# The key half of a cross attention's projection, computed three stages earlier and parked in DRAM

## The chip, the cores and the metric

The kernel runs on one core of one Trainium2 chip. The metric is device time in microseconds of one launch. Five engines run their own instruction streams in order and meet only through semaphores: TensorE (PE, matmuls), VectorE (DVE), ScalarE (ACT), GpSimd (POOL) and SyncE (SP, which here only issues the weight loads). The DMA engines move data beside them.

## What is computed

Two transformer blocks on 256 tokens of width 2048, all in float32. The parts that matter here, in the order of the kernel's stages:

```python
mix = concatenate([rmsnorm(u, conv_out_norm), rmsnorm(attn, attn_out_norm)]) @ w_out     # stage w_out
x = x + rmsnorm(mix, post_mix_norm)                                                      # the addition after it
hf = rmsnorm(x, pre_ffn_norm)
ff = (silu(hf @ w_gate) * (hf @ w_up)) @ w_down                                          # ffn, down
x = x + rmsnorm(ff, post_ffn_norm)
...                                            # qkv_a, mix2b (delta rule, block attention), w_out_2
q = rmsnorm_2(x, xattn_norm_g) @ w_xq          # stage xq
kv = rmsnorm_2(mem, mem_norm_g) @ w_xkv        # stage xkv: mem is an input, 256 x 2048
k, v = split(kv)                               # 4 heads of 128 each
o = softmax(q k^T * 128**-0.5) v               # cross attention
x = x + o @ w_xo                               # xo, then ffn_2, down_2
```

`mem` is an input, so keys and values of the cross attention depend on nothing that the kernel computes before.

## The kernel before

Every product is a `Gemm` object in the list `GEMMS`. It has groups of weight tiles; one tile is 512 rows by 512 columns of a weight (1 MB), and it is worked off as two units of 256 rows each. A float32 product is made from split operands: `split_act` (L441) writes the rounded high part `w_hi` of a unit on ACT, `split_dve` (L447) writes the rest `w_lo` on DVE, and PE multiplies high by both parts of the activations and low by the high part. The high parts go through a ring of `HIS = 4` units: ACT cannot split unit u before PE has finished unit u-4. The raw tiles go through a ring of `RAW = 4` tiles that SP fills in the order of `GEMMS`.

Activations are split in the same way into `x2` (tile `x` in the trace) by `prep_act` (L923, L925: high parts, "rows" below) and `prep_dve` (L938, L940: low parts), two of the 16 chunks of 128 channels at a time. `square_act` (L969) and `reduce_dve` (L688, L690) gather the sum of squares for a norm, four chunks at a time; PE adds over partitions with a matmul against ones (L1029, L1050, L1060, L1063); `root` (ACT, L1081 to L1084) and `refine` (DVE, L1095 to L1107) make the reciprocal root. The scale of a norm is applied to a product's columns when they leave the accumulator, so a product may start before its norm is known; the addition after w_out may not, since the residual stream must be finished first.

The order on ACT and DVE is written out by hand in their blocks. `ahead` splits units 0 to 2 of the next product, evicts the last group of the one before and splits unit 3; `run`/`turn` split the others, one at a time, and call one step of a `filler` generator after each. Two places matter.

Between w_out and the gate (the first group of ffn), PE's last w_out unit is followed by the sums for the norm "mix". Then `refine` and `add_norm` on DVE scale the product (L2252), add it to `xt` (L2433) and write the low parts of `x2`, while `ready_act` does ACT's share. PE's first gate unit needs the first two chunks of `x2`, each later one two more.

In xkv both halves are multiplied from `xm2` (tile `xm` in the trace), the split `mem`, which is prepared during w_out_2: first the keys, as a wide group of four tiles (L799, L802), then the values in swapped form (L785 to L788). The filler there is `prep_steps_act` and `prep_steps_dve` for "xq": eight steps, each of two chunks of the finished `xt` with its squares, one step after each split from unit 4 on. Nothing of it can start before w_out_2 has ended, since `x2` is in use until then and `xt` is not final. Stage xq follows, and needs those chunks. POOL issues the load of `mem` (L2293), and the small transfers that turn the norm's row into a column for the values (`column_pool`, L1540, L1542).

Of the kernel before, what the change touches and what calls it, by code (L numbers as in the profile page):

```python
# [17 lines left out]
F32 = mybir.dt.float32  # L18
# [6 lines left out]
P = 128  # L25
T = 256
# [118 lines left out]
def build(nc, A, out):  # L145
    with ExitStack() as ctx:
# [68 lines left out]
        wide_tmp = sb("wide_tmp", [P, 8, T], F32, a_gate)  # L215

        XK, XVN, XQ, XO = 0, 8, 12, 16
        XM = 20
# [49 lines left out]
        def x2c(k):  # L268
            return x2[:, k]

        def h2c(k):
# [11 lines left out]
                           for h0, n, off, width, at in ((0, 4, 0, 128, 0), (4, 4, 0, 128, 4), (0, 8, 128, 64, 8))],  # L283
# [3 lines left out]
                            for h0 in (4, 0)],  # L287
# [17 lines left out]
                 x2c, rs_x, form="narrow", column=1),  # L305
            Gemm("w_out_2", 2, [group(w_loop(A["w_out_2"], b * P, 2 * W), 4, out=(xt, 0 + b, 8), kind="add")
                        for b in (0, 4)], x2c),
            Gemm("xkv", 1, [group(w_cols(A["w_xkv_2"], 0, W), 4, out=(ar, XK, 0)),
                           group(w_cols(A["w_xkv_2"], W, W), 4, out=(ar, XVN, XH // 2), kind="v")], lambda k: xm2[:, k], rs_x, column=2),
            Gemm("xq", 1, [group(w_cols(A["w_xq_2"], 0, W), 4, out=(ar, XQ, 0))], x2c, rs_x),  # L310
            Gemm("xo", 1, [group(w_cols(A["w_xo_2"], 512 * n, W), 1, out=(xt, 4 * n, 0), kind="add")
                           for n in range(4)], x2c),
# [12 lines left out]
        for n, g in enumerate(GEMMS):  # L325
            g.before = GEMMS[n - 1] if n else None
            g.u0, g.p0, g.e0, g.g0, g.f0, g.slot0 = tiles, prods, ops, groups, hidden, list(slots)
            at = 0
            g.per_unit = []
            if g.name not in ("latents", "ukv", "down", "down_2"):  # L330

                side = 1 if g.name in ("uq", "qkv_a") else 0
            for k, gr in enumerate(g.groups):
                gr["form"] = "swap" if gr["kind"] == "v" else g.form
                gr["t"], gr["e"], gr["n"] = at, 2 * k, k - (3 if g.name == "w_out" else 0)
                if gr["banks"] is None:
# [24 lines left out]
            hidden += g.turns if g.name.startswith("ffn") else 0  # L361
# [195 lines left out]
        def evict_dve(dve, g, i, gr):  # L557
# [197 lines left out]
        def multiply(pe, g, *stats, between=None, filler=None, at=FIRST + 1):  # L755
# [70 lines left out]
            if between:  # L826
                at, extra = between
                body(0, 0, at)
                extra()
                body(0, at)  # L830
            elif g.name == "w_out":
                at = g.units - 2
                body(0, 0, at)
                pe.wait_ge(geared, 12)
                sum_rows(pe, "mix")
                body(0, at)
                sum_quarter(pe, "mix", STATS["mix"][2] - 1)
            else:
                body(0)
            if g.name in STREAM_STAT and g.turns == 2:  # L840
# [23 lines left out]
        for name, n, first in [("x", 16, 0), ("q", 6, 0), ("kv", 4, 6), ("attn", 8, 8), ("conv", 8, 0),  # L864
                               ("ffn", 16, 0), ("mix2", 16, 0), ("gdn", 8, 0), ("moba", 8, 8), ("mem", 16, 0),
                               ("xq", 16, 0), ("xo", 4, 0), ("ffn2", 16, 0)]:
            PREPS[name] = (sum(c for _, c, _ in PREPS.values()), n, first)
# [23 lines left out]
            return lambda k: (x_lo, off + min(k, total))  # L891

        for name, preps in [("conv_in", ["x"]), ("latents", ["x"]), ("uq", ["q"]), ("ukv", ["kv"]),
                            ("w_out", ["attn", "conv"]), ("ffn", ["ffn"]), ("qkv_a", ["mix2"]), ("mix2b", ["mix2"]),
                            ("w_out_2", ["gdn", "moba"]), ("xkv", ["mem"]), ("xq", ["xq"]),
                            ("xo", ["xo"]), ("ffn_2", ["ffn2"])]:
            G[name].needs = needs_of(*preps)
# [9 lines left out]
            halves += g.turns * g.halves  # L907


        PREP_TO = {"mem": xm2, "q": xq1}  # L910

        def prep_act(act, name, src, gain, ready=None, square=None, after=None, c0=0, count=None):

# [96 lines left out]

        SUM_AT = {"kv": 2, "mean": 2}

        SUM_BANK = {name: 3 if name in ("q", "kv", "mix", "ff", "mix2", "final") else 7 for name in STATS}
        POST_GAIN = {"mix": "post_mix", "ff": "post_ffn"}

        def sum_out(name):
# [1255 lines left out]
        def _(pool):  # L2272
# [53 lines left out]
        def _(act):  # L2326
# [39 lines left out]
            filler = conv_norms_act(act)  # L2366
            next(filler)
            run_("w_out", filler)
            ahead_("ffn")
            root(act, "mix")  # L2370
            ready_act(act, "ffn", gain_of("pre_ffn"), lambda c: (x_added, c + 1), "w_out", G["ffn"])
            run_("ffn", stat=["ffn"], done=DC // 2)
            ahead_("down")
            run_("down")
            ahead_("qkv_a")
# [13 lines left out]
            run_("w_out_2", prep_steps_act(act, "mem", mem_src, gain_of("mem"), lambda c: (mem_in, 16),  # L2389
                                           first=(x_lo, PREPS["moba"][0] + PREPS["moba"][1])))  # L2390
            ahead_("xkv")
            filler = prep_steps_act(act, "xq", xs, gain_of("xattn"), banks_out("w_out_2"), "w_out_2")
# [22 lines left out]
        def _(dve):  # L2415
# [38 lines left out]
                assert apply.n == n0 + ADDS  # L2454


            for u in range(DC // 2):
                split_dve(dve, G["conv_in"], 0, u)
                if u == 0:
# [23 lines left out]
            filler = conv_norms_dve(dve)  # L2483
            next(filler)
            run_("w_out", filler)
            ahead_("ffn")
            add_norm("mix", mix_out, "ffn", "pre_ffn", G["ffn"])
            run_("ffn", stat=["ffn"], done=DC // 2)
            ahead_("down")
            run_("down")  # L2490
            ahead_("qkv_a")
# [39 lines left out]
        def _(pe):  # L2531
# [29 lines left out]
            attention_pe(pe, ATTN["cross"], [lambda e: e.wait_ge(*groups_out("xq")()), lambda e: e.wait_ge(*all_evicted("xkv")())])  # L2561
# [59 lines left out]
```

## Time and profile before

| | us |
|---|---|
| median of three runs | 2622.0 (2620.73 to 2622.4) |
| the profiled execution | 2621.72 |
| its span, first to last instruction | 2619.9 |
| PE busy in the span | 2520.7 (96%) |
| DVE busy | 1658.8 (63%) |
| ACT busy | 1266.8 (48%) |
[...]

The span is cut into 40 slices of 65.5 us in the page's second section; PE stands at 8 or 9 tenths in every one. Times below are us from the span's start. w_out runs from 302 to 407, the gate starts at 417.8, xkv runs from 1736.2 to 1782.5 and xq follows. A number in brackets at the end of a timeline row is the engine's idle time before the row, with the instruction that ended it. Rows of one kind overlap by some 0.1 us in the trace, so the distance between two starts is what an instruction costs in a sequence; it is shorter than the printed duration.

### The profile page before, as it was taken

To read this page: it belongs to the slowest core of one execution; us is meant where nothing else is said; L and a number is where in the kernel's file an instruction comes from. 1 tells how busy PE (TensorE), PEld (TensorE's weight loads), DVE (VectorE), ACT (ScalarE), POOL (GpSimd) and SP (SyncE) were. 2 spreads that over 40 slices of the span, in tenths; PEclk is the share of its full clock that TensorE was granted. 3 is DMA by queue.
4 is the path that set the end of the run, shared out by engine and by line. 5 is a ranking of instruction groups with operands and counts; after the bars stand their busy time and mean duration, and the time that the engine had idled before them with its cause. 6 is when DMAs were issued, how large, how long until landed. Compare 5 with 4: busy or idle time off the path is not lost.

```text
span 2619.9 us, 37766 instructions
## 1 busy us (share of the span) xinstructions
PE 2520.7 (96%) x14866; PEld 2210.0 (84%) x14866; DVE 1658.8 (63%) x2173; ACT 1266.8 (48%) x1627; POOL 62.7 (2%) x57
## 2 busy tenths in 40 slices
PE   8999898999999999989999999998999999999997
PEld 7877697888888888878889989886888888888886
DVE  6898756666656554547776436765767676665454
ACT  5455555444444443445453345654644545444342
POOL 0000000000000000000003210000000000000000
PEclk9999899999999999999999999999999999999999
DMA  6553144655565555544542235453455555565553
GB/s 240 176 145 113 49 158 132 193 183 186 191 191 185 185 192 176 193 161 154 183 164 97 97 121 177 161 181 125 153 186 191 192 184 186 190 192 187 183 184 122
DMA packets 236033, 436.26 MB, mean 167 GB/s; under 512 B 14408, under 2 KB 32856, under 8 KB 235792
## 3 DMA queue, kind: packets, MB, share of 16 engines
q1 hardware_dynamic: 232384, 423.66, 49.9%
q0 software_dynamic: 2240, 6.80, 0.8%
q10 hardware_dynamic: 1296, 4.19, 0.4%
q8 instruction: 82, 1.34, 0.2%
q14 instruction: 31, 0.25, 0.0%
HBM read 432.51 MB, written 3.69 MB: 166 GB/s over the span
## 4 chain that ended last, share of the span: by engine, by line
PE 88%; DVE 7%; ACT 3%; issue 1%; DMA 1%; SPq 0%; DVEq 0%; ACTq 0%
PE ps L799 46%; PE ps L802 23%; PE ps L808 3%; PE ps L810 3%; PE ps L811 3%; DVE w_lo L447 2%; DVE ar L1219 1%; PE ps L1479 1%; PE ps L785 1%; ACT w_hi L441 1%; PE ps L788 1%; PE ps L787 1%; PE ps L1252 1%; PE ps L2086 1%; PE ps L2092 1%
## 5 line engine op out<-in xcount | busy, mean ns | idle before, releaser
L447 DVE TENSOR_TENSOR w_lo<-w_raw,w_hi 128x1024 fp32r<-128x1024 f32 (+3 forms) x820 | 994.3, 1217 | 774.4 <-ACT w_hi L441 772.3
L799 PE MATMUL ps<-x,w_hi 128*128 128x512 f32 x4064 | 1289.4, 399 | 44.5 <-issue 19.4
L441 ACT ACTIVATE w_hi<-w_raw 128x1024 fp32r<-128x1024 f32 (+3 forms) x820 | 853.4, 1045 | 921.8 <-PE ps L802 801.9
L802 PEld LDWEIGHTS ps<-x,w_lo 128*128 128x128 f32 x4064 | 769.9, 189 | 182.9
L802 PE MATMUL ps<-x,w_lo 128*128 128x256 f32 x4064 | 803.3, 279 | 0.0
L799 PEld LDWEIGHTS ps<-x,w_hi 128*128 128x128 f32 x4064 | 625.1, 190 | 48.3 <-issue 36.7
L799 PE MATMUL ps<-h,w_hi 128*128 128x512 f32 x1408 | 444.2, 397 | 4.3 <-DVE w_lo L447 4.3
L802 PEld LDWEIGHTS ps<-h,w_lo 128*128 128x128 f32 x1408 | 265.4, 188 | 62.9
L802 PE MATMUL ps<-h,w_lo 128*128 128x256 f32 x1408 | 277.3, 278 | 0.0
L799 PEld LDWEIGHTS ps<-h,w_hi 128*128 128x128 f32 x1408 | 215.0, 189 | 5.1 <-DVE w_lo L447 4.9
L808 PE MATMUL ps<-x,w_hi 128*128 128x256 f32 x640 | 188.5, 294 | 8.1 <-issue 6.3
L810 PE MATMUL ps<-x,w_hi 128*128 128x256 f32 x640 | 182.8, 286 | 0.0
L811 PE MATMUL ps<-x,w_lo 128*128 128x256 f32 x640 | 182.7, 286 | 0.0
L487 ACT ACTIVATE half<-ps 128x512 f32<-128x512 f32 (+1 forms) x162 | 94.4, 592 | 91.6 <-PE ps L802 91.6
L808 PEld LDWEIGHTS ps<-x,w_hi 128*128 128x128 f32 x640 | 124.7, 195 | 13.6 <-issue 10.3
L810 PEld LDWEIGHTS ps<-x,w_hi 128*128 128x128 f32 x640 | 124.7, 195 | 0.3
L811 PEld LDWEIGHTS ps<-x,w_lo 128*128 128x128 f32 x640 | 124.5, 195 | 0.0
L1219 DVE SCALAR_TENSOR_TENSOR ar<-ar,cols 128x255 f32<-128x255 f32 (+29 forms) x180 | 73.7, 467 | 0.6
L925 ACT ACTIVATE x<-xt,cols 128x256 fp32r<-128x256 f32 x80 | 35.5, 496 | 26.4 <-DVE xt L2433 26.4
L940 DVE SCALAR_TENSOR_TENSOR x<-xt,cols,x 128x256 fp32r<-128x256 f32 x80 | 34.8, 480 | 3.8 <-ACT x L925 3.8
L620 DVE TENSOR_TENSOR up<-half,ps 128x512 f32<-128x512 f32 x44 | 30.1, 684 | 10.9 <-ACT half L487 10.9
L620 DVE TENSOR_TENSOR gate<-half,ps 128x512 f32<-128x512 f32 x44 | 30.0, 684 | 10.5 <-ACT half L487 10.5
(307 smaller groups left out, 1710.5 us busy)
## 6 DMA issues: line engine op xcount, KB each, us to landing
w_raw<-in_w_gate SPq DMA_DIRECT2D x88, 1024.0 KB, 5.1
w_raw<-in_w_up SPq DMA_DIRECT2D x88, 1024.0 KB, 5.2
w_raw<-in_w_down SPq DMA_DIRECT2D x88, 1024.0 KB, 5.1
w_raw<-in_w_in SPq DMA_DIRECT2D x79, 1024.0 KB, 5.1
w_raw<-in_w_out SPq DMA_DIRECT2D x32, 1024.0 KB, 5.1
w_raw<-in_w_xkv SPq DMA_DIRECT2D x8, 1024.0 KB, 5.0
w_raw<-in_w_uq SPq DMA_DIRECT2D x18, 256.0 KB, 3.7
w_raw<-in_w_ukv SPq DMA_DIRECT2D x16, 256.0 KB, 3.9
```

The lines of the kernel that those rows point to most:

```text
L441: nc.scalar.activation(w_hi[:, u % HIS, 0:ks.stop - ks.start, cs], w_raw[:, slot(g, j), ks, cs], ACT.Copy)\
L447: nc.vector.tensor_tensor(w_lo[:, slot(g, j), ks, cs], w_raw[:, slot(g, j), ks, cs], w_hi[:, u % HIS, 0:ks.stop - ks.start, cs].bitcast(F3 ...
L487: nc.scalar.activation(half[:, c:c + n, h], banks[:, :, h], ACT.Copy).then_inc(half_out, 1)
L620: nc.vector.tensor_tensor(dst(c, n)[:, :, h], half[:, c:c + n, h], banks[:, :, T + h.start:T + h.stop], ALU.add)\
L799: nc.tensor.matmul(bank, w_h(k, cs), x(k).rearrange("p a n -> p (a n)"), start=(n == 0 and k == 0), stop=False)
L802: ins = nc.tensor.matmul(bank[:, T:2 * T], w_l(k, cs), x(k)[:, 0, :], start=False, stop=(final and k == ks.stop - 1))
L808: nc.tensor.matmul(out_m, w_h(k, cs), x(k)[:, 0, :], start=(first and k == 0 and m % 2 == 0), stop=False)
L810: nc.tensor.matmul(out_m, w_h(k, cs), x(k)[:, 1, :], start=False, stop=False)
L811: ins = nc.tensor.matmul(out_m, w_l(k, cs), x(k)[:, 0, :], start=False, stop=(final and k == ks.stop - 1 and last_m))
L925: ins = nc.scalar.activation(x2[:, first + c, 0, :], src(c), ACT.Copy, scale=gain(c))
L940: ins = nc.vector.scalar_tensor_tensor(x2[:, first + c, 1, :], src(c), gain(c), hi, ALU.mult, ALU.subtract)
L1219: nc.vector.scalar_tensor_tensor(y[:, s:T], u[:, 0:T - s], w, y[:, s:T], ALU.mult, ALU.add).then_inc(tap1, 1)
```

## The change

The keys' product becomes a stage of its own, `xk`, between w_out and ffn. For it `mem` is loaded once more, earlier (a POOL DMA of 2 MB after the first attention), and split into `xm2` by eight filler steps at the end of w_out. The product is evicted without a scale (kind "raw") to `ar`, written by POOL to a DRAM tensor `xk_d` (512 KB), and read back during w_out_2. After the xq steps DVE multiplies it by `rs_x`, the reciprocal root of mem's norm, which is only computed in xkv. `mem` is loaded and split a second time for the values. Stage xkv keeps four tiles. ACT and DVE wait for the end of the write to DRAM (`xk_out`) before gate unit 5, because ffn's hidden activations overwrite the place. The addition after w_out, `add_norm("mix", ...)`, is replaced by `add_mix`, with the splits of xk's units 4 to 7 and the gate's units 0 to 4 between its parts. The sums of "mix" follow xk's unit 0 on PE. Bank assignments of some products and sums swap sides.

```diff
+            Gemm("xk", 1, [group(w_cols(A["w_xkv_2"], 0, W), 4, out=(ar, XS, 0), kind="raw")], lambda k: xm2[:, k]),
...
-            Gemm("xkv", 1, [group(w_cols(A["w_xkv_2"], 0, W), 4, out=(ar, XK, 0)),
-                           group(w_cols(A["w_xkv_2"], W, W), 4, out=(ar, XVN, XH // 2), kind="v")], lambda k: xm2[:, k], rs_x, column=2),
+            Gemm("xkv", 1, [group(w_cols(A["w_xkv_2"], W, W), 4, out=(ar, XVN, XH // 2), kind="v")], lambda k: xm2[:, k], rs_x, column=2),
...
-                side = 1 if g.name in ("uq", "qkv_a") else 0
+                side = 1 if g.name in ("uq", "ffn", "qkv_a", "xq") else 0
...
+        def w_out_act(act):
+
+            yield from conv_norms_act(act)
+            for c in range(0, DC, 2):
+                prep_act(act, "memk", mem_src, gain_of("mem"), lambda c: (mem_in, 16), None, None, c, 2)
+                yield
...
+            pool.wait_ge(conv_pe, 2)
+            pool.wait_ge(x_lo, PREPS["attn"][0] + PREPS["attn"][1])
+            pool.dma_start(ar[:, MEM:MEM + DC, :], A["mem"]).then_inc(mem_in, 16)
+            pool.wait_ge(evicted, G["xk"].e0 + 2)
+            pool.dma_start(xk_d, ar[:, XS:XS + XH, :]).then_inc(xk_out, 16)
...
+            pool.wait_ge(applied, gated_done)
+            pool.wait_ge(xk_out, 16)
+            pool.dma_start(ar[:, XK:XK + XH, :], xk_d).then_inc(xk_back, 16)
             column_pool(pool, 2, rs_x, "mem")
...
+            g, nxt = G["xk"], G["ffn"]
+            split_act(act, g, 0, 4)
             root(act, "mix")
...
+            rows(0, 2, "w_out")
+            for u in range(5, 8):
+                split_act(act, g, 0, u)
+                rows(2 * u - 8, 2)
+            square_act(act, "ffn", 0, xs, 4)
+            for u in range(4):
+                if u == FIRST:
+                    finish(evict_act(act, g, 0, g.groups[-1]))
+                split_act(act, nxt, 0, u)
+                rows(8 + 2 * u, 2)
+                if u % 2:
+                    square_act(act, "ffn", 1 + u // 2, xs, 4)
+            split_act(act, nxt, 0, 4)
+            square_act(act, "ffn", 3, xs, 4)
+            act.wait_ge(xk_out, 16)
+            run_("ffn", stat=["ffn"], done=5)
...
+                split_dve(dve, g, 0, 4)
+                refine(dve, "mix")
+                add(0, 2)
+                low(0, 2)
+                split_dve(dve, g, 0, 5)
+                add(2, 2)
+                low(2, 2)
+                split_dve(dve, g, 0, 6)
+                add(4, 4)
+                low(4, 2)
+                split_dve(dve, g, 0, 7)
+                low(6, 2)
+                split_dve(dve, nxt, 0, 0)
+                add(8, 4)
+                low(8, 2)
+                reduce_dve(dve, "ffn", 0, 4)
+                split_dve(dve, nxt, 0, 1)
+                low(10, 2)
+                split_dve(dve, nxt, 0, 2)
+                add(12, 2)
+                low(12, 2)
+                finish(evict_dve(dve, g, 0, g.groups[-1]))
+                reduce_dve(dve, "ffn", 1, 4)
+                split_dve(dve, nxt, 0, FIRST)
+                add(14, 2)
+                low(14, 2)
+                reduce_dve(dve, "ffn", 2, 4)
+                split_dve(dve, nxt, 0, 4)
...
             run_("xkv", filler, stat=["mem"])
             finish(filler)
+            dve.wait_ge(xk_back, 16)
+            k = ar[:, XK:XK + XH, :]
+            nc.vector.tensor_tensor(k, k, bc(rs_x, XH), ALU.mult).then_inc(xk_scaled, 1)
             ahead_("xq")
...
+            multiply(pe, G["xk"], between=(1, lambda: sum_quarter(pe, "mix", STATS["mix"][2] - 1)))
             multiply(pe, G["ffn"], "ffn", at=DC // 2)
```

DVE's program in stage xkv before, from the reciprocal root of mem's norm on (`x_50` is `x2`, two chunks a step; `gate` and `up` hold squares; L620 and L631 evict and scale the keys):

```order
L1107 SCALAR_TENSOR_TENSOR rs_x<-st_v,st_y 128x256
L447 TENSOR_TENSOR w_lo<-w_raw,w_hi 128x1024
L940 SCALAR_TENSOR_TENSOR x_50<-xt,cols,x_50 128x256 x2
L447 TENSOR_TENSOR w_lo<-w_raw,w_hi 128x1024
L940 SCALAR_TENSOR_TENSOR x_50<-xt,cols,x_50 128x256 x2
L688 TENSOR_TENSOR up<-up 128x512
L690 TENSOR_TENSOR ssq<-up 128x256
L447 TENSOR_TENSOR w_lo<-w_raw,w_hi 128x1024
L940 SCALAR_TENSOR_TENSOR x_50<-xt,cols,x_50 128x256 x2
L447 TENSOR_TENSOR w_lo<-w_raw,w_hi 128x1024
L940 SCALAR_TENSOR_TENSOR x_50<-xt,cols,x_50 128x256 x2
```

And the same place after the change, from the second pair of chunks behind the root on:

```order
L941 SCALAR_TENSOR_TENSOR x_50<-xt,cols,x_50 128x256 x2
L690 TENSOR_TENSOR up<-up 128x512
L692 TENSOR_TENSOR ssq<-up 128x256
L941 SCALAR_TENSOR_TENSOR x_50<-xt,cols,x_50 128x256 x4
L690 TENSOR_TENSOR gate<-gate 128x512
L692 TENSOR_TENSOR ssq<-gate 128x256
L941 SCALAR_TENSOR_TENSOR x_50<-xt,cols,x_50 128x256 x4
L690 TENSOR_TENSOR up<-up 128x512
L692 TENSOR_TENSOR ssq<-up 128x256
L2603 TENSOR_TENSOR ar<-ar,rs_x 128x1024
L447 TENSOR_TENSOR w_lo<-w_raw,w_hi 128x1024 x3
```

The last eight chunks, their reduces and the keys' scale now stand in one piece after xkv's last split and ahead of xq's first.

DVE's program between w_out and the gate before, from the first addition of four chunks on:

```order
L2252 TENSOR_TENSOR ar<-ar,st_y 128x1024
L2433 TENSOR_TENSOR xt<-xt,ar 128x1024
L940 SCALAR_TENSOR_TENSOR x_50<-xt,cols,x_50 128x256 x4
L2252 TENSOR_TENSOR ar<-ar,st_y 128x1024
L2433 TENSOR_TENSOR xt<-xt,ar 128x1024
L940 SCALAR_TENSOR_TENSOR x_50<-xt,cols,x_50 128x256 x2
L447 TENSOR_TENSOR w_lo<-w_raw,w_hi 128x1024
L940 SCALAR_TENSOR_TENSOR x_50<-xt,cols,x_50 128x256 x2
L447 TENSOR_TENSOR w_lo<-w_raw,w_hi 128x1024
```

And after the change, from the same addition on:

```order
L2269 TENSOR_TENSOR ar<-ar,st_y 128x1024
L2511 TENSOR_TENSOR xt<-xt,ar 128x1024
L941 SCALAR_TENSOR_TENSOR x_50<-xt,cols,x_50 128x256 x2
L447 TENSOR_TENSOR w_lo<-w_raw,w_hi 128x1024
L941 SCALAR_TENSOR_TENSOR x_50<-xt,cols,x_50 128x256 x2
L447 TENSOR_TENSOR w_lo<-w_raw,w_hi 128x1024
L2269 TENSOR_TENSOR ar<-ar,st_y 128x1024
L2511 TENSOR_TENSOR xt<-xt,ar 128x1024
L941 SCALAR_TENSOR_TENSOR x_50<-xt,cols,x_50 128x256 x2
L690 TENSOR_TENSOR gate<-gate 128x512
L692 TENSOR_TENSOR ssq<-gate 128x256
L447 TENSOR_TENSOR w_lo<-w_raw,w_hi 128x1024
```

Of the splits there, the first is xk's unit 7, the second the gate's unit 0 and the third the gate's unit 1; before, the two splits are the gate's units 4 and 5, since units 0 to 3 were split ahead of the addition.

## Rows read from the trace of the kernel before

**Rows 1.** PE's timeline at the gate: start, us, instruction, idle before.

```profile
407.47 1.98 PE L1050 MATMUL ps<-up,ones 128*128 128x256 f32 x8
417.81 1.19 PE L799 MATMUL ps<-x,w_hi 128*128 128x512 f32 x2 [8.36 <-issue]
...
422.96 0.62 PE L799 MATMUL ps<-x,w_hi 128*128 128x512 f32 x2
...
443.82 1.89 PE L1060 MATMUL ps<-up,ones 128*128 128x256 f32 x8
```

**Rows 2.** DVE's timeline from the end of w_out to the gate's unit 5.

```profile
411.12 0.42 DVE L1095 TENSOR_SCALAR st_v<-ps 128x256 f32<-128x256 f32 x1
...
413.84 0.42 DVE L2252 TENSOR_TENSOR ar<-ar,st_y 128x256 f32<-128x256 f32 x1
...
415.84 0.68 DVE L2252 TENSOR_TENSOR ar<-ar,st_y 128x512 f32<-128x512 f32 x1
...
423.77 1.22 DVE L2252 TENSOR_TENSOR ar<-ar,st_y 128x1024 f32<-128x1024 f32 x1
425.10 1.23 DVE L2433 TENSOR_TENSOR xt<-xt,ar 128x1024 f32<-128x1024 f32 x1
426.90 0.88 DVE L940 SCALAR_TENSOR_TENSOR x<-xt,cols,x 128x256 fp32r<-128x256 f32 x2 [0.58 <-ACT x L925]
428.25 1.23 DVE L447 TENSOR_TENSOR w_lo<-w_raw,w_hi 128x1024 fp32r<-128x1024 f32 x1 [0.47 <-ACT w_hi L441]
429.39 0.87 DVE L940 SCALAR_TENSOR_TENSOR x<-xt,cols,x 128x256 fp32r<-128x256 f32 x2
...
431.32 0.69 DVE L688 TENSOR_TENSOR gate<-gate 128x512 f32<-128x512 f32 x1
...
432.38 1.22 DVE L2252 TENSOR_TENSOR ar<-ar,st_y 128x1024 f32<-128x1024 f32 x1
```

**Rows 3.** ACT's timeline beside it.

```profile
426.36 0.91 ACT L925 ACTIVATE x<-xt,cols 128x256 fp32r<-128x256 f32 x2 [2.07 <-DVE xt L2433]
```

**Rows 4.** PE's timeline in w_out, at a short wait.

```profile
347.01 0.39 PE L808 MATMUL ps<-x,w_hi 128*128 128x256 f32 x1 [1.79 <-DVE w_lo L447]
```

**Rows 5.** Stretches: us; busy PE, PEld, DVE, ACT, POOL; PEclk; DMA share; GB/s.

```profile
350.00:351.00 1.00, 1.00 (x7) 1.00 (x6) 0.36 (x1) 0.00 (x0) 0.00 (x0) 0.50 0.00 0
350.00:390.00 40.00, 40.00 (x332) 40.00 (x331) 19.21 (x20) 22.31 (x32) 0.00 (x0) 0.99 0.48 159
```

**Rows 6.** PE's timeline in xkv.

```profile
1736.20 0.63 PE L799 MATMUL ps<-xm,w_hi 128*128 128x512 f32 x2
...
1747.34 1.89 PE L1029 MATMUL ps<-ssq,ones 128*128 128x256 f32 x8
1748.89 0.81 PE L799 MATMUL ps<-xm,w_hi 128*128 128x512 f32 x2
...
1760.22 0.40 PE L785 MATMUL ps<-w_hi,xm 128*128 128x512 f32 x1
...
1782.53 0.62 PE L799 MATMUL ps<-x,w_hi 128*128 128x512 f32 x2
```

**Rows 7.** DVE's timeline in xkv.

```profile
1758.08 1.22 DVE L447 TENSOR_TENSOR w_lo<-w_raw,w_hi 128x1024 fp32r<-128x1024 f32 x1
...
1764.13 1.28 DVE L620 TENSOR_TENSOR ar<-half,ps 128x512 f32<-128x512 f32 x2
```

**Rows 8.** ACT's timeline in xkv.

```profile
1755.14 1.04 ACT L969 ACTIVATE up<-xt 128x1024 f32<-128x1024 f32 x1
```

**Rows 9.** PE's timeline at w_out's start.

```profile
302.44 0.55 PE L808 MATMUL ps<-x,w_hi 128*128 128x256 f32 x1 [6.27 <-issue]
...
306.82 0.28 PE L811 MATMUL ps<-x,w_lo 128*128 128x256 f32 x1
```

**Rows 10.** The page's sixth section, DMA issues: KB each, us to landing.

```profile
out_t<-tx ACTq DMA_DIRECT2D x4, 512.0 KB, 2.6
masks_s<-in_masks POOLq DMA_DIRECT2D x1, 512.0 KB, 4.5
```

More of the change, by code:

```diff
@@ L217, in build @@
         XK, XVN, XQ, XO = 0, 8, 12, 16
-        XM = 20
+        XS = 16
         rel_hot = sb("rel_hot", [BUCKETS, 384], F32, a_gate)
@@ L621, in evict_dve @@
                     .then_inc(evicted, 1)
+            if kind == "raw":
+                return
             if kind == "sum":
@@ L836, in multiply @@
                 body(0, at)
-                sum_quarter(pe, "mix", STATS["mix"][2] - 1)
             else:
@@ L863, in build @@
         PREPS = {}
-        for name, n, first in [("x", 16, 0), ("q", 6, 0), ("kv", 4, 6), ("attn", 8, 8), ("conv", 8, 0),
+        for name, n, first in [("x", 16, 0), ("q", 6, 0), ("kv", 4, 6), ("attn", 8, 8), ("conv", 8, 0), ("memk", 16, 0),
                                ("ffn", 16, 0), ("mix2", 16, 0), ("gdn", 8, 0), ("moba", 8, 8), ("mem", 16, 0),
@@ L893, in build @@
         for name, preps in [("conv_in", ["x"]), ("latents", ["x"]), ("uq", ["q"]), ("ukv", ["kv"]),
-                            ("w_out", ["attn", "conv"]), ("ffn", ["ffn"]), ("qkv_a", ["mix2"]), ("mix2b", ["mix2"]),
+                            ("w_out", ["attn", "conv"]), ("xk", ["memk"]), ("ffn", ["ffn"]), ("qkv_a", ["mix2"]), ("mix2b", ["mix2"]),
                             ("w_out_2", ["gdn", "moba"]), ("xkv", ["mem"]), ("xq", ["xq"]),
@@ L907, in build @@
             halves += g.turns * g.halves
-        PREP_TO = {"mem": xm2, "q": xq1}
+        PREP_TO = {"mem": xm2, "memk": xm2, "q": xq1}
         def prep_act(act, name, src, gain, ready=None, square=None, after=None, c0=0, count=None):
@@ L1011, in build @@
         SUM_AT = {"kv": 2, "mean": 2}
-        SUM_BANK = {name: 3 if name in ("q", "kv", "mix", "ff", "mix2", "final") else 7 for name in STATS}
+        SUM_BANK = {name: 4 if name == "mix" else 3 if name in ("q", "kv", "ffn", "mix2", "xq", "final") else 7 for name in STATS}
         POST_GAIN = {"mix": "post_mix", "ff": "post_ffn"}
@@ L1533, in build @@
         mask_in = sem("mask_in")
+        xk_d = nc.dram_tensor("xk_d", [P, XH, T], F32, kind="Internal").ap()
+        xk_out, xk_back, xk_scaled = sem("xk_out"), sem("xk_back"), sem("xk_scaled")
         rs_d = nc.dram_tensor("rs_d", [3, T], F32, kind="Internal").ap()
@@ L2247, in attention_rest_dve, with w_out_dve @@
                 yield
+        def w_out_act(act):
[3 more added lines that the diff above has]
+                yield
+        def w_out_dve(dve):
+            yield from conv_norms_dve(dve)
+            for c in range(0, DC, 2):
+                prep_dve(dve, "memk", mem_src, gain_of("mem"), None, c, 2)
+                yield
         def apply(dve, src, n, first=0):
@@ L2293, in _ @@
             pool.dma_start(ar[:, MEM:MEM + DC, :], A["mem"]).then_inc(mem_in, 16)
+            gated_done = 6 + 2 * ADDS + 2
+            pool.wait_ge(applied, gated_done)
+            pool.wait_ge(xk_out, 16)
+            pool.dma_start(ar[:, XK:XK + XH, :], xk_d).then_inc(xk_back, 16)
             column_pool(pool, 2, rs_x, "mem")
@@ L2365, in _ @@
             prep_act(act, "attn", attn_src, gain_of("attn_out"), lambda c: (applied, 1 if c < 2 else 2), None, "ukv")
-            filler = conv_norms_act(act)
+            filler = w_out_act(act)
             next(filler)
             run_("w_out", filler)
-            ahead_("ffn")
+            finish(filler)
+            ahead_("xk")
+            g, nxt = G["xk"], G["ffn"]
+            split_act(act, g, 0, 4)
             root(act, "mix")
-            ready_act(act, "ffn", gain_of("pre_ffn"), lambda c: (x_added, c + 1), "w_out", G["ffn"])
-            run_("ffn", stat=["ffn"], done=DC // 2)
+            rows = lambda c, n, after=None: prep_act(act, "ffn", xs, gain_of("pre_ffn"), lambda c: (x_added, c + 1), None, after, c, n)
+            rows(0, 2, "w_out")
[14 more added lines that the diff above has]
+            run_("ffn", stat=["ffn"], done=5)
             ahead_("down")
@@ L2388, in _ @@
             prep_act(act, "moba", moba_src, lambda c: col("moba_norm"), lambda c: (hn_used, 16))
-            run_("w_out_2", prep_steps_act(act, "mem", mem_src, gain_of("mem"), lambda c: (mem_in, 16),
+            run_("w_out_2", prep_steps_act(act, "mem", mem_src, gain_of("mem"), lambda c: (mem_in, 32),
                                            first=(x_lo, PREPS["moba"][0] + PREPS["moba"][1])))
@@ L2454, in add_norm, with add_mix, add @@
                 assert apply.n == n0 + ADDS
+            def add_mix():
+                g, nxt = G["xk"], G["ffn"]
+                low = lambda c, n: prep_dve(dve, "ffn", xs, gain_of("pre_ffn"), None, c, n)
+                def add(c0, n):
+                    dve.wait_ge(geared, c0 + n)
+                    apply(dve, mix_out, n, c0)
+                    x = xt[:, c0:c0 + n, :]
+                    nc.vector.tensor_tensor(x, x, span(mix_out, c0, n), ALU.add).then_inc(x_added, n)
+                n0 = apply.n
+                split_dve(dve, g, 0, 4)
[26 more added lines that the diff above has]
+                split_dve(dve, nxt, 0, 4)
+                assert apply.n == n0 + ADDS
             for u in range(DC // 2):
@@ L2482, in _ @@
             prep_dve(dve, "attn", attn_src, gain_of("attn_out"))
-            filler = conv_norms_dve(dve)
+            filler = w_out_dve(dve)
             next(filler)
             run_("w_out", filler)
-            ahead_("ffn")
-            add_norm("mix", mix_out, "ffn", "pre_ffn", G["ffn"])
-            run_("ffn", stat=["ffn"], done=DC // 2)
+            finish(filler)
+            ahead_("xk")
+            add_mix()
+            dve.wait_ge(xk_out, 16)
+            run_("ffn", stat=["ffn"], done=5)
             ahead_("down")
@@ L2560, in _ @@
             pe.wait_ge(st_done, STATS["xq"][0] + 1)
-            attention_pe(pe, ATTN["cross"], [lambda e: e.wait_ge(*groups_out("xq")()), lambda e: e.wait_ge(*all_evicted("xkv")())])
+            attention_pe(pe, ATTN["cross"], [lambda e: e.wait_ge(*groups_out("xq")()), lambda e: e.wait_ge(*all_evicted("xkv")()),
+                                             lambda e: e.wait_ge(xk_scaled, 1)])
             multiply(pe, G["xo"])
```

## The prediction, written before the changed kernel ran

> **What bounds the kernel now.** The table of the page first: PE is busy for 96% of the span, so the time is PE's work plus PE's gaps, and a change that leaves PE's work alone can only win or lose gaps. So the second view is PE's timeline at the two places where the keys' product leaves and arrives. Between w_out and the gate the sums for the norm run from 407.47, and the first gate matmul starts at 417.81 after 8.36 us of idleness [rows 1]. Around it there is more. The clock is low when PE returns: the first 5.15 us (417.81 to 422.96) carry four groups of matmuls that at full clock take an eighth of 22.3 us, 2.8 us, so 2.4 us are lost. A unit costs 2.79 us ((1747.34 - 1736.20)/4, [rows 6]); eight take 22.3, but the gate's eight last 26.0 (417.81 to 443.82), so 1.3 us more go into a later wait. The whole stretch from 407.47 to 443.82 is 36.35 us, with 22.3 of work in it [rows 1]. At the other place there is no gap: the keys run from 1736.20 and, after the sums (1.55 us), to 1760.22, the values to 1782.53, and xq follows at once [rows 6].
>
> **What moves on PE.** The keys' 22.3 us leave xkv and come in behind w_out. Nothing is added to PE's work. Two questions remain: how much of the gap they fill, and whether xkv's other half still covers what the keys covered there.
>
> **Place one, the gate.** DVE has a serial chain here, and the change puts more into it than it takes out of PE's way. Prices in a sequence, by starts: reciprocal root 2.72 (411.12 to 413.84); an addition of four chunks 2.56 (423.77 to 425.10 + 1.23), of two 1.47 (two instructions of the length of the one at 415.84, with their link); after an addition ends, the low parts of two chunks and one split take 3.06 (426.33 to 429.39), since both wait for ACT in turn; a split alone 1.14; two low parts alone 0.8; a reduce 1.06 (431.32 to 432.38) [rows 2]. On ACT two high parts take 0.8 in a sequence, and a square or split 0.95 [rows 3, 8]. The eviction of the keys takes 1.2 [rows 7].
>
> The chain starts later than before. xk's unit 4 can be split only when PE has finished unit 0, at 407.47 + 2.79 = 410.3; ACT and then DVE split it, and DVE reads the sum at 412.75 instead of 411.12. First addition at 415.5. From there, in the written order: add 2, low and split (xk 5) to 420.0; the same (xk 6) to 424.5; add 4, low and split (xk 7) to 430.15; low; the gate's unit 0 is split by 432.85, after ACT's square. Then add 4, low, reduce, split of gate unit 1: 439.0. Low and the split of unit 2, again behind an ACT square: 441.15. Add 2, low, eviction, reduce, split of unit 3: 447.4. Add 2, low, reduce behind the third square, split of unit 4: 452.95.
>
> PE beside it: xk 0 to 410.3, sums to 411.8, xk 1 to 6 without a stop to 428.6, 1.5 us of waiting for xk 7, done at 432.95, gate 0 to 435.75; then 3.2 us, 2.85 us and 2.75 us of waiting before gate units 1, 3 and 4. From unit 4 on the splits come every 1.14 us, faster than PE's 2.79, so gate unit 8's place is reached at 452.95 + 4 x 2.79 = 464.1. With 22.3 us more work, break-even would be 443.82 + 22.3 = 466.1. So the gap of 8.4 us is filled, but it comes back in four pieces, and the gain is 2.0 us at full clock.
>
> Do the pieces cost the clock too? [...] The price lies between 0 and the 2.4 us of the gap before; I take 1.0. [...] Gain at place one: 1.0, with -3 to +5 as its bounds (other rounding of ACT's and DVE's hand-overs, some 0.3 us at each of ten).
>
> Other parts at this place. The eight added steps of `mem` at the end of w_out cost DVE and ACT some 7 us each, where both are busy only 19 and 22 of 40 us and PE waits for neither [rows 5]: nothing; without that cover it would be 7. The load of 2 MB runs beside weight loads at a DMA share of 0.48 over that stretch: nothing, at most 2 us if a tile came late. The write of 512 KB starts after the eviction at 445.2. Its price isn't in the trace; 512 KB landed in 2.6 us from ACT's queue and 4.5 from POOL's [rows 10]. So it ends at about 450, before ACT and DVE reach the wait at 452.7 and 453. Behind the wait the splits of gate units 5 and up are queued, for which PE has until 455.7: nothing, and 4 us if it took three times as long. [...]
>
> **Place two, xq.** The eight xq steps (16 high and low parts, four squares, four reduces) had twelve splits to lie between, and now have four. DVE's stream is the same up to the second reduce, which ends at 1758.08 [rows 7]. ACT is free at 1756.1 [rows 8]. What is left of the steps then stands in one piece: eight low parts 3.2, two reduces 2.1, to 1763.4, ACT just ahead of them. Then the scale of the keys, a 128x1024 product like the one at 423.77, 1.14 in a sequence: 1764.55. Then xq's unit 0 is split: 1765.7. PE ends the values at 1736.20 + 22.3 + 1.55 = 1760.05. So it waits 5.65 us where it waited for nothing. The wait is like the 6.27 us at w_out's start, after which PE ran at low speed from 302.44 to 306.82; half of these 4.4 us is lost, 2.2 [rows 9]. xq's other splits (1.14 each, with the values' eviction of 1.3 before the fourth) come before PE's need. The keys' old eviction and scale (2.4 us of DVE) were hidden before and free nothing now. Place two costs 5.65 + 2.2 = 7.8; bounds 5.5 and 9.5. The read of the keys from DRAM is issued a hundred us earlier: nothing.
>
> **Sum.** -1.0 + 7.8 = +6.8 us. The profiled execution, 2621.72, becomes 2628.5 (span 2626.7). The median lies 0.3 above it: 2628.8.
>
> **Rivals.**
> - The gap is really filled (the other side). If ACT and DVE keep ahead of PE between w_out and the gate, 12.0 us go (8.4 + 2.4 + 1.3), and with 7.8 lost later it is -4.2: 2617.8. It decides if gate unit 1 is split by 434, when PE without any stop ends unit 0, rather than at 439. For it: DVE is idle for 37% of the span. Against it: from 412.75 on DVE carries the root (2.7), eight splits (9.1), six additions (11.0), sixteen low parts (6.4), three reduces (3.2) and an eviction (1.2), 33.6 us before any wait for ACT, while PE's work from there to gate unit 4 is 29.7.
> - The xq steps are hidden after all, and place two costs 1 or less: 2622. It would need the last eight chunks to be ready before the values end. Against it: every term of that piece is an instruction of DVE's own, none a wait.
> - The write to DRAM ends last at the gate, at 457 or later: +4 us, 2632.8.
> - The keys' transfer is nothing and the product is done twice: no; the diff takes the group out of xkv.
>
> **Chances.** Forecast 0.66, filled gap 0.10, hidden steps 0.09, late write 0.15. What a measurement of this kernel can tell from no change is about 0.2%, 5.2 us: 2616.8 to 2627.2 is "same". The forecast at +6.8 with some 2.5 us of spread leaves a quarter of its chance under that bound; with the first and second rivals, less the part of the first that goes beyond -5.2, I say slower 0.62, same 0.31, faster 0.07. Range: 2620.5, where the second rival reaches in, to 2633.5, which holds the late write. The forecast's own range is 2625 to 2632.
>
> **What would show it.** Right: PE's idle time of about 5 to 6 us before the first xq matmul, released by DVE's w_lo, with PEclk 0.50 behind it; three or four waits of 1.5 to 3.5 us for DVE's w_lo between 428 and 453 instead of one of 8.4; ffn's sums (then L1061) at 463 to 467. The write landing within 5 us. Wrong: sums at 458 or earlier (the gap is filled), a wait for `xk_out` at ACT or DVE, or xq starting within 2 us of the values' end.

## The result, and the profile after

The changed kernel takes 2630.34 us (median of 7 runs, 2625.46 to 2634.16), against 2622.0 (7 runs beside them, 2619.68 to 2624.81). The ratio is 1.0033, with a 95% interval of 1.0022 to 1.0043: slower by 8.3 us. The forecast was 2628.8 in a range of 2620.5 to 2633.5.

The page of the profile after, its first and fourth sections:

```profile
PE 2527.5 (96%) x14866; PEld 2214.4 (84%) x14866; DVE 1664.7 (63%) x2189; ACT 1273.0 (48%) x1643; POOL 64.3 (2%) x60
...
PE 88%; DVE 7%; ACT 3%; issue 1%; DMA 1%; DVEq 0%; SPq 0%; ACTq 0%
```

As before, PE is busy for 96%. Shares of the span can't show a change of 0.3%; the two places can.

**Place one, w_out to ffn's sums.** PE's timeline after, which answers to [rows 1]: start, us, instruction, idle before with what ended it. The sums at 409.62 now stand behind unit 0 of the keys, so w_out ended 2.79 us before them, at 406.83.

```profile
409.62 1.89 PE L1051 MATMUL ps<-up,ones 128*128 128x256 f32 x8
...
429.76 0.73 PE L801 MATMUL ps<-xm,w_hi 128*128 128x512 f32 x2 [1.52 <-DVE w_lo L447]
...
438.58 1.09 PE L801 MATMUL ps<-x,w_hi 128*128 128x512 f32 x2 [2.98 <-DVE w_lo L447]
...
447.10 0.73 PE L801 MATMUL ps<-x,w_hi 128*128 128x512 f32 x2 [1.10 <-DVE w_lo L447]
...
452.70 1.22 PE L801 MATMUL ps<-x,w_hi 128*128 128x512 f32 x2 [2.56 <-DVE w_lo L447]
...
465.37 1.89 PE L1061 MATMUL ps<-up,ones 128*128 128x256 f32 x8
```

The gap of 8.36 us is gone, and four waits of 8.2 us in all stand in its place, each ended by DVE's low part of the weights. From w_out's end to ffn's sums it is 465.37 - 406.83 = 58.54 us; less the keys' 22.3, 36.24. Before it was 36.35 [rows 1]. The place gains 0.1 us. The forecast had a gain of 2.0 at full clock and took 1.0 of it off for the clock.

DVE's timeline there, which answers to [rows 2], with the low parts that gate units 1, 3 and 4 wait for:

```profile
412.11 0.42 DVE L1096 TENSOR_SCALAR st_v<-ps 128x256 f32<-128x256 f32 x1
...
414.84 0.69 DVE L2269 TENSOR_TENSOR ar<-ar,st_y 128x512 f32<-128x512 f32 x1
...
437.30 1.22 DVE L447 TENSOR_TENSOR w_lo<-w_raw,w_hi 128x1024 fp32r<-128x1024 f32 x1
...
445.82 1.22 DVE L447 TENSOR_TENSOR w_lo<-w_raw,w_hi 128x1024 fp32r<-128x1024 f32 x1
...
451.43 1.22 DVE L447 TENSOR_TENSOR w_lo<-w_raw,w_hi 128x1024 fp32r<-128x1024 f32 x1
```

Each of the three begins about 1.3 us ahead of the PE row that it releases (437.30 and 438.58, 445.82 and 447.10, 451.43 and 452.70). The chain runs as forecast: counted from w_out's end, gate unit 4 starts at 45.9 us, where the working had 45.5.

The rest is the clock. Two stretches after: us; busy PE, PEld, DVE, ACT, POOL; PEclk; DMA share; GB/s.

```profile
453.00:454.00 1.00, 1.00 (x4) 0.81 (x4) 0.73 (x1) 1.00 (x2) 0.00 (x0) 0.50 1.07 418
456.00:457.00 1.00, 1.00 (x8) 0.87 (x7) 0.77 (x1) 0.00 (x0) 0.00 (x0) 1.00 0.00 0
```

Behind the last wait PE's granted clock is 0.50 (full speed is 1.00), with 4 matmul records in a us where 8 stand later. From 452.70 to the sums it takes 12.67 us for four units of 2.79: 1.5 us are lost there. PE doesn't wait again before the sums, so nothing hides its slow start. (It was slow behind the wait of 2.98 us too, from 438.58 to 442.33, with a clock of 0.50 at 439 to 442; there the next low part came later still.)

**Place two, xkv to xq.** PE's timeline after, which answers to [rows 6]:

```profile
1759.19 0.40 PE L787 MATMUL ps<-w_hi,xm 128*128 128x512 f32 x1
...
1770.08 1.89 PE L1030 MATMUL ps<-ssq,ones 128*128 128x256 f32 x8
...
1782.49 0.39 PE L790 MATMUL ps<-w_lo,xm 128*128 128x512 f32 x1
1788.49 1.22 PE L801 MATMUL ps<-x,w_hi 128*128 128x512 f32 x2 [5.61 <-DVE w_lo L447]
...
1802.18 1.89 PE L1030 MATMUL ps<-ssq,ones 128*128 128x256 f32 x8
```

PE now waits 5.61 us for xq's first unit, where it followed without a gap. Between the two rows of sums lie 32.10 us (1770.08 to 1802.18). In before they were at 1747.34 [rows 6] and 1793.67, 46.33 apart, and less the keys' 22.3 that is 24.0: the place costs 8.1 us. The second of these rows in before:

```profile
1793.67 1.89 PE L1029 MATMUL ps<-ssq,ones 128*128 128x256 f32 x8
```

DVE's timeline in that wait, which answers to [rows 7]:

```profile
1780.79 1.67 DVE L941 SCALAR_TENSOR_TENSOR x<-xt,cols,x 128x256 fp32r<-128x256 f32 x4
1782.38 0.68 DVE L690 TENSOR_TENSOR gate<-gate 128x512 f32<-128x512 f32 x1
...
1783.43 1.66 DVE L941 SCALAR_TENSOR_TENSOR x<-xt,cols,x 128x256 fp32r<-128x256 f32 x4
1785.02 0.68 DVE L690 TENSOR_TENSOR up<-up 128x512 f32<-128x512 f32 x1
...
1786.08 1.22 DVE L2603 TENSOR_TENSOR ar<-ar,rs_x 128x1024 f32<-128x1024 f32 x1
1787.21 3.49 DVE L447 TENSOR_TENSOR w_lo<-w_raw,w_hi 128x1024 fp32r<-128x1024 f32 x3
```

No row has a wait in brackets: DVE is working through the xq steps and the keys' scale, and the first of the three splits ends some 7.6 us after 1780.79. Forecast was 1758.08 to 1765.7, also 7.6. Behind the wait PE ran slowly again:

```profile
1788.00:1792.00 4.00, 3.51 (x10) 3.01 (x11) 4.00 (x6) 0.00 (x0) 0.00 (x0) 0.50 0.00 0
```

**What cost nothing.** The page's sixth section, which answers to [rows 10]: both transfers of the keys. The write is issued at 445.14 and lands after 4.4 us, before ACT and DVE come to their wait for it, and no row there waits for `xk_out`.

```profile
xk_d<-ar POOLq DMA_DIRECT2D x1, 512.0 KB, 4.4
...
ar<-xk_d POOLq DMA_DIRECT2D x1, 512.0 KB, 4.7
```

The two places together give -0.1 + 8.1 = +8.0 us; the medians differ by 8.3. The profiled execution is longer still, 2634.16 against 2621.72. It is the longest of its seven. Of its excess of 12.4 us, 8.0 lie in the two places and 3.4 between xq's sums and ffn_2's, where no instruction was changed: 81.70 us, against 78.33 in before's. More on that at the end.

### The profile page after: what moved, and what is told of

Read it like the earlier page. It is cut to its first block, busy times and chain, and to the rows that moved or that the text cites. A ratio compares the mean times of both kernels' runs of the same rounds, so it can differ in the third digit from the quotient of the medians.

```text
span 2632.4 us, 37807 instructions
## 1 busy us (share of the span) xinstructions
PE 2527.5 (96%) x14866; PEld 2214.4 (84%) x14866; DVE 1664.7 (63%) x2189; ACT 1273.0 (48%) x1643; POOL 64.3 (2%) x60
## 4 chain that ended last, share of the span: by engine, by line
PE 88%; DVE 7%; ACT 3%; issue 1%; DMA 1%; DVEq 0%; SPq 0%; ACTq 0%
PE ps L801 46%; PE ps L804 23%; PE ps L810 3%; PE ps L812 3%; PE ps L813 3%; DVE w_lo L447 2%; DVE ar L1220 1%; ACT w_hi L441 1%; PE ps L1480 1%; PE ps L787 1%; PE ps L790 1%; PE ps L789 1%; PE ps L1253 1%; PE ps L2089 1%; PE ps L2095 1%
## 5 line engine op out<-in xcount | busy, mean ns | idle before, releaser
L487 ACT ACTIVATE half<-ps 128x512 f32<-128x512 f32 x162 | 94.5, 592 | 93.7 <-PE ps L804 93.6
L620 DVE TENSOR_TENSOR up<-half,ps 128x512 f32<-128x512 f32 x44 | 30.1, 684 | 10.9 <-ACT half L487 10.9
L620 DVE TENSOR_TENSOR gate<-half,ps 128x512 f32<-128x512 f32 x44 | 30.0, 684 | 10.5 <-ACT half L487 10.5
```

The lines of the kernel that those rows point to most:

```text
L487: nc.scalar.activation(half[:, c:c + n, h], banks[:, :, h], ACT.Copy).then_inc(half_out, 1)
```

## Experiments

The theory: place two costs some 8 us because the values' four tiles don't cover the xq steps, and place one gains nothing because DVE's chain is as long as PE's work and the clock takes the rest. The rivals: the time goes to the keys' scale or transfer, to the eight added `mem` steps, or to something that the moved product does wherever it stands. Each kernel was timed beside before on the same chip: e1, e2, e3 and e6 on one, where before took 2624.75 us (median of 23 runs), and e4, e5 and e7 on another, where it took 2623.97 (24 runs). The expectations count from the first before, 2622.0, so a ratio has to be multiplied by 2622.0 before it is held against them.

**e1: before, with the keys' product left out.** The keys are not computed at all. It asks for place two alone.

```diff
-            Gemm("xkv", 1, [group(w_cols(A["w_xkv_2"], 0, W), 4, out=(ar, XK, 0)),
-                           group(w_cols(A["w_xkv_2"], W, W), 4, out=(ar, XVN, XH // 2), kind="v")], ...
+            Gemm("xkv", 1, [group(w_cols(A["w_xkv_2"], W, W), 4, out=(ar, XVN, XH // 2), kind="v")], ...
```

> The kernel before with the keys' product left out of xkv and nothing in its place (the keys of the cross attention are not computed); xq uses the other banks, as in the changed kernel. The gate is as before, so only place two is seen. Theory (the xq steps had the keys' product as cover): 22.3 us of PE work go, but PE waits some 4.5 us for DVE's w_lo before xq (5.6 less the scale of the keys, 1.14, which isn't there) and loses about 2 us to the low clock: -22.3 + 6.6, so 2606.3. Rival (the steps are hidden): -22.3, so 2599.7, no wait before xq.

Measured: 2607.07 us (2604.85 to 2609.17), ratio 0.9938 (0.9924 to 0.9951), so 16.3 us less for 22.3 us of work gone. PE's timeline before xq:

```profile
1764.80 0.93 PE L798 MATMUL ps<-x,w_hi 128*128 128x512 f32 x2 [4.43 <-DVE w_lo L446]
```

The wait is there with no load from DRAM and no scale: 4.43 us of the 5.61. The scale, 1.14 us of DVE, is the difference. The stretch between the sums is 30.11 us, 6.1 above before's 24.0, and 22.3 - 6.1 = 16.2 is the measured gain. The keys' work was cover for 6.1 us.

**e2: after, with the keys multiplied a second time in xkv.** It keeps the new place one and gives place two its cover back; no load from DRAM and no scale.

```diff
+            Gemm("xkv", 1, [group(w_cols(A["w_xkv_2"], 0, W), 4, out=(ar, XK, 0)),
...
-            pool.dma_start(ar[:, XK:XK + XH, :], xk_d).then_inc(xk_back, 16)
...
-            nc.vector.tensor_tensor(k, k, bc(rs_x, XH), ALU.mult).then_inc(xk_scaled, 1)
```

> The changed kernel, but xkv multiplies the keys again as before and the cross attention uses these; the copy in DRAM is written and not read. The product is there twice, place two is as before, so only the gate and the end of w_out are seen. Theory (DVE's chain eats the gap): +22.3 us of PE work, less a gain at the gate of 0 to 1 us: 2643 to 2644.5. Rival (the gap of 12 us is filled, and the loss is elsewhere): 2632.

Measured: 2642.64 us (2639.94 to 2645.19), ratio 1.0076 (1.0062 to 1.009), +19.9 us (16.3 to 23.6). No wait before xq, and the gate as in after:

```profile
428.88 0.73 PE L802 MATMUL ps<-xm,w_hi 128*128 128x512 f32 x2 [1.53 <-DVE w_lo L448]
437.70 1.21 PE L802 MATMUL ps<-x,w_hi 128*128 128x512 f32 x2 [2.97 <-DVE w_lo L448]
446.23 0.73 PE L802 MATMUL ps<-x,w_hi 128*128 128x512 f32 x2 [1.10 <-DVE w_lo L448]
451.84 1.22 PE L802 MATMUL ps<-x,w_hi 128*128 128x512 f32 x2 [2.56 <-DVE w_lo L448]
```

The added product costs its own 22.3 us, within the interval, though it stands in a gap of 8 us. By the interval alone up to 6 us could have been won at the gate. The stretches say less: from w_out's end to ffn's sums it is 58.50 us, 36.2 without the keys' 22.3 against 36.35 before, and between the sums at xq 46.33, as in before. Place one gains about nothing.

**e3: after, with xq's first splits laid between the last xq steps, and the keys' scale behind them.** If place two is a matter of order on DVE, its whole cost goes.

```diff
             run_("xkv", filler, stat=["mem"])
+            ahead_("xq", filler=filler)
             finish(filler)
             dve.wait_ge(xk_back, 16)
             ...
-            ahead_("xq")
```

> The changed kernel with one order changed on ACT and DVE: after xkv's last split, the splits of xq's units 0 to 2 stand between the xq steps 5 to 7, and the last step and the keys' scale stand behind split 3. Nothing is taken out. Theory: DVE's w_lo for xq's unit 0 is ready at about the values' end, the wait of 5.6 us and the low clock behind it go: 7 to 8 us less than the changed kernel, about 2622 to 2623. Rival (the loss is not the piece but the number of steps, or the clock in the attention behind it): less than 3 us come back, 2627 or more.

Measured: 2621.37 us (2616.8 to 2625.22), ratio 0.9992 (0.9983 to 1.0002). PE goes from the values straight into xq:

```profile
1779.02 0.39 PE L790 MATMUL ps<-w_lo,xm 128*128 128x512 f32 x1
1779.24 0.62 PE L801 MATMUL ps<-x,w_hi 128*128 128x512 f32 x2
```

DVE there: xq's first splits at 1777.30 and 1779.23, while the last chunks and the scale come after them.

```profile
1777.30 1.22 DVE L447 TENSOR_TENSOR w_lo<-w_raw,w_hi 128x1024 fp32r<-128x1024 f32 x1
...
1779.23 1.22 DVE L447 TENSOR_TENSOR w_lo<-w_raw,w_hi 128x1024 fp32r<-128x1024 f32 x1
...
1788.46 1.22 DVE L2604 TENSOR_TENSOR ar<-ar,rs_x 128x1024 f32<-128x1024 f32 x1
```

Between the sums it is 23.81 us, as before the change (24.0). So all 8.1 us of place two were one wait and its clock, and the wait was an order: xq's first units need the first chunks alone, and were split behind the last. The ratio makes it 2619.9 on the scale of the expectation, 2 to 3 us under it. In the profiled execution 1.4 us of that is the clock at the gate, which the last section shows; how often it falls so in the others isn't known.

**e6: before, with the early load of `mem` and its eight steps in w_out.** No product, so these parts stand alone.

```diff
+            pool.dma_start(ar[:, MEM:MEM + DC, :], A["mem"]).then_inc(mem_in, 16)
...
-            filler = conv_norms_act(act)
+            filler = w_out_act(act)
...
+            finish(filler)
```

> The kernel before with the early load of mem (2 MB) and its eight steps on ACT and DVE at the end of w_out added, without a product that uses them. Theory: hidden, 2622 within 1 us, w_out's sums at 407 as before. Rival: DVE and ACT or the load delay w_out, up to +7.

Measured: 2623.81 us (2618.16 to 2625.88), ratio 0.9997 (0.9985 to 1.0008). w_out's sums come at 406.14, at 407.47 in before [rows 1]. The steps and the load are hidden, within the 3 to 4 us that the interval leaves; the sums come no later.

**e4: after, with a shorter chain ahead of the gate.** Three reduces, two of the squares and the keys' eviction go behind the split of gate unit 4, and the wait for the write moves to unit 9.

```diff
                 low(8, 2)
-                reduce_dve(dve, "ffn", 0, 4)
                 split_dve(dve, nxt, 0, 1)
...
                 low(12, 2)
-                finish(evict_dve(dve, g, 0, g.groups[-1]))
-                reduce_dve(dve, "ffn", 1, 4)
                 split_dve(dve, nxt, 0, FIRST)
                 add(14, 2)
                 low(14, 2)
-                reduce_dve(dve, "ffn", 2, 4)
                 split_dve(dve, nxt, 0, 4)
+                reduce_dve(dve, "ffn", 0, 4)
+                finish(evict_dve(dve, g, 0, g.groups[-1]))
```

> The changed kernel with DVE's chain between w_out and the gate made shorter: the three reduces and the eviction of the keys stand behind the split of the gate's unit 4 instead of between the parts (ACT's squares and the eviction's copies likewise), units 5 to 7 are split between them, and the wait for the write to DRAM stands at the gate's unit 9. The same instructions, another order. Theory (DVE's chain sets the gate): the four pieces, 1.2 + 3 x 1.06 us less what waits for ACT take up, leave the chain before unit 4, so the sums (L1061) come 3 to 4 us earlier and the time is about 2626 to 2627. Rival (PE or ACT sets it, or the write to DRAM): no change, 2630.

Measured: 2628.23 us (2625.01 to 2631.14), ratio 1.0018 (1.0009 to 1.0027). The waits:

```profile
438.88 0.73 PE L801 MATMUL ps<-x,w_hi 128*128 128x512 f32 x2 [2.64 <-DVE w_lo L447]
...
450.86 0.73 PE L801 MATMUL ps<-x,w_hi 128*128 128x512 f32 x2 [1.50 <-DVE w_lo L447]
...
454.25 0.73 PE L801 MATMUL ps<-x,w_hi 128*128 128x512 f32 x2 [0.32 <-DVE w_lo L447]
...
462.72 1.89 PE L1061 MATMUL ps<-up,ones 128*128 128x256 f32 x8
```

The row for gate unit 1 falls only from 2.98 to 2.64, since DVE without the reduce waits 1.40 us for ACT's high part instead:

```profile
437.60 1.23 DVE L447 TENSOR_TENSOR w_lo<-w_raw,w_hi 128x1024 fp32r<-128x1024 f32 x1 [1.40 <-ACT w_hi L441]
```

The wait of 2.56 before unit 4 becomes 1.50, with 0.32 more before unit 5, and full speed behind both (a clock of 1.00 from 451 to 458). The stretch (from w_out's end, 407.46) is 55.26 us instead of 58.54: 3.3 us, nearly half of it (1.5) the clock. With the keys' 22.3 us taken off, 3.4 of before's 36.35 are won, not the 12 of the first rival. It is the stretch that shows this: the interval of e4's ratio overlaps that of after's repetition on the same chip (e7, 1.0018 to 1.0039). How much each of the pieces that were put off gives wasn't tried.

**e5: e3 and e4 together.**

> Both reorderings together, of the gate's chain and of xq's first splits. Theory: they add up, -4 and -7.5 against the changed kernel: 2618 to 2620, which would be less than both kernels. Rival (the gain at one place is given back at the other through the clock): 2622 or more.

Measured: 2617.83 us (2614.12 to 2620.05), ratio 0.9978 (0.9969 to 0.9987): faster than both kernels. The gate's stretch is 55.26 us again, and xq's 23.78. The ratio gives 2616.2 on the scale of the expectation, some 2 us under it. Filling the gap is worth some 3.5 us by the traces, if place two is paid for by order.

**e7: after, once more beside e4 and e5.**

> The changed kernel once more, on the same chip as the two reorderings, since its runs spread over 2625 to 2634. Theory: 2630 within 2, and the wait before xq of 5.6 us in every profile, while attention and xo behind it differ by some 3 us with the clock. Rival: the wait itself varies from run to run.

Measured: 2631.27 us (2628.32 to 2633.22), ratio 1.0029 (1.0018 to 1.0039). The gate's stretch is 58.54 again; between the sums at xq it is 32.33, with this wait:

```profile
1784.34 1.22 PE L801 MATMUL ps<-x,w_hi 128*128 128x512 f32 x2 [5.59 <-DVE w_lo L447]
```

All eight in one table. Each stretch is less 22.3 us where the keys' product is in it, and read against before's (36.35 and 24.0); the sum of the two is set against the timed difference, the ratio less one times before's median.

| | gate | xq | sum | timed, us (95%) |
|---|---|---|---|---|
| after | -0.1 | +8.1 | +8.0 | +8.7 (+5.8 to +11.3) |
| e7, after again | -0.1 | +8.3 | +8.2 | +7.6 (+4.7 to +10.2) |
| e1, no keys | 0.0 | +6.1 | -16.2, with -22.3 of work | -16.3 (-19.9 to -12.9) |
| e2, product twice | -0.1 | 0.0 | +22.2, with +22.3 of work | +19.9 (+16.3 to +23.6) |
| e3, xq's order | -1.5 | -0.2 | -1.7 | -2.1 (-4.5 to +0.5) |
| e4, gate's chain | -3.4 | +7.4 | +4.0 | +4.7 (+2.4 to +7.1) |
| e5, both | -3.4 | -0.2 | -3.6 | -5.8 (-8.1 to -3.4) |
| e6, steps only | -0.3 | 0.0 | -0.3 | -0.8 (-3.9 to +2.1) |

All sums lie in their intervals, e5's near the edge of its own. The wait before xq is 5.6 us in after, e7 and e4, and the clock behind it took 2.5, 2.8 and 1.9 us more: that is most of why the three differ in the second column.

## Why the prediction came out right

- **Place two was the change, and was sized nearly right.** Forecast: 5.65 us of wait and 2.2 for the clock. Measured: 5.61 and, of the 8.1, the other 2.5. e1, with 4.43 us for want of cover alone, and e3, with none after a change of order alone, show both halves of the argument: the keys' work was DVE's cover, and the order of DVE's piece set the price.
- **Place one was mis-sized.** The term "The price lies between 0 and the 2.4 us of the gap before; I take 1.0" was too small: 1.5 us are lost behind the wait of 2.56 us alone, and with 0.4 of DVE being later than worked out the gain was 0.1, not 1.0. It is a size, not a mechanism: the four waits came where they were said to (forecast 1.5, 3.2, 2.85, 2.75; measured 1.52, 2.98, 1.10, 2.56). The third was short because PE, slow behind the second (0.50 at 439 to 442), came to its unit late: two units from 438.58 to 446.00 took 7.4 us instead of 5.6. How much of the gap's 2.4 us short waits would cost was the author's estimate. One short wait was read ahead of the run: 1.79 us in w_out, with a clock of 0.50 at 350 to 351 [rows 4, 5]. Had the full 2.4 us been paid, the gain would have been about nil, and in after, e2 and e7 it was (stretches of 58.54, 58.50 and 58.54 us). But in after the clock took 1.5 us of it and not 2.4, and PE was at full speed behind the waits of 1.52 and 1.10 us (1.00 at 430 to 432 and at 447 to 450). In e3, behind a wait of 2.56 us at the same unit, the clock stayed up (1.00 at 453 to 454) and the stretch was 57.16.
- **A term that the working doesn't list.** Its steps to 439.0, 447.4 and 452.95 are 0.6, 0.6 and 1.1 us longer than the listed prices add up to. The difference is DVE's wait for ACT's high parts after an addition, 0.58 us in [rows 2], and at the last step the wait for ACT's square. After shows them there too, 0.58 us each and 0.46 for the square, so the steps were right though a reader can't add them up.
- **The filled gap did not come, for the reason given.** The rival wanted gate unit 1 split by 434; its low part began at 437.30. e4 shows how much of it order can win: 3.4 us.
- **The hidden parts were hidden.** The steps and the load (e6, 0.9997); the write, by 4.4 us to landing and no wait behind it. So the late write did not come. Its chance of 0.15 was the author's estimate, and no run shows a late completion: the 512 KB written took 4.4 us to land, where POOL's load of 512 KB took 4.5 [rows 10].
- **The total.** The sum was 6.8, and 8.0 by its terms as measured: 0.9 of the difference is place one, 0.3 place two.

## What to carry to other kernels

A product that is moved takes its cover with it: before it leaves, list what the other engines did beside it, and put what the next product needs first ahead of what it needs last. A gap of PE that stood for a serial chain on another engine did not fill here with work that needs the same engine. It broke into short waits, and only the reordering that put off what no one waits for won something. The same can be expected, though it wasn't tried elsewhere, where the added work lengthens the chain that the gap stands for. Work out the ledger by stretches between two fixed instructions, less the work moved, since it agreed with the timed ratios in every run here, while the total of one profiled execution can mislead: after's was 12.4 us above before's, with 8.3 between the medians.

## What the runs showed of the hardware

**A wait of the same length doesn't always lower the clock.** Behind a wait of 2.56 us for gate unit 4, in after (452.70) and e3 (452.24), the stretch from 453 to 454 shows 0.50 in after, above, and in e3:

```profile
453.00:454.00 1.00, 1.00 (x8) 0.86 (x7) 1.00 (x2) 1.00 (x2) 0.00 (x0) 1.00 1.04 406
```

It is worth 1.4 us (58.54 against 57.16). The programs are the same up to there, but PE had not run alike just before. PE's timeline in e3:

```profile
438.11 1.22 PE L801 MATMUL ps<-x,w_hi 128*128 128x512 f32 x2 [2.97 <-DVE w_lo L447]
...
446.63 0.73 PE L801 MATMUL ps<-x,w_hi 128*128 128x512 f32 x2
...
452.24 0.73 PE L801 MATMUL ps<-x,w_hi 128*128 128x512 f32 x2 [2.56 <-DVE w_lo L447]
```

The low clock behind the wait before unit 1 lasted longer in e3 (0.50 up to 444, in after up to 442), so that PE came to unit 3 as its split did and the wait of 1.10 us wasn't there. The stretch from 443 to 444, in after and then in e3:

```profile
443.00:444.00 1.00, 1.00 (x8) 0.87 (x7) 1.00 (x3) 1.00 (x4) 0.00 (x0) 1.00 0.00 0
```

```profile
443.00:444.00 1.00, 1.00 (x5) 0.90 (x4) 1.00 (x3) 1.00 (x3) 0.00 (x0) 0.50 0.00 0
```

Which of these differences kept the clock up is not shown. At xo's start two executions part with no difference close by. PE's rows in the last 6.35 us ahead of xo's first matmul are alike in before and e7, all at full speed (a clock of 1.00), and so is the wait of 1.62 us. The first matmul behind it is at full speed in before, 0.70 us with a clock of 1.00, and at half speed in e7, 1.19 us with 0.50. PE's timeline of before and then of e7:

```profile
1828.42 0.70 PE L1327 MATMUL ps<-ar 128*128 128x256 f32 x2 [0.69 <-ACT ar L1374]
...
1831.17 0.70 PE L799 MATMUL ps<-x,w_hi 128*128 128x512 f32 x2 [1.62 <-issue]
```

```profile
1832.21 0.70 PE L1328 MATMUL ps<-ar 128*128 128x256 f32 x2 [0.69 <-ACT ar L1375]
...
1834.96 1.19 PE L801 MATMUL ps<-x,w_hi 128*128 128x512 f32 x2 [1.62 <-issue]
```

Of the nine profiles five have PE at full speed ahead of this wait: it stayed there in two (before and e2) and fell in three (e3, e4 and e7). In the other four, after among them, it was slow already (0.50).

The stretch from xq's sums to ffn_2's, about 80 us, took 77.04 to 81.70 us over the executions profiled here. Such places are a likely part of the spread of one kernel (before ran from 2618.3 to 2627.76 over 23 runs on one chip); that they make up all of it was not shown. It is why differences of 2 us are read here from stretches and not from the total of one execution.
